# Routing of the expert layer: shifted, gained and transposed rows, positions and lists computed in another form and order

## The reference, cut to what matters

```python
h2 = rmsnorm(x, g_norm2) * (1.0 + sc2) + sh2
logits = h2 @ w_router + b_router              # 32 experts
top_logit, top_idx = lax.top_k(logits, 4)
gate = softmax(top_logit)
# every expert's tokens, padded to blocks of 128 slots:
padded = (counts + 127) // 128 * 128
slot = pad_start[expert] + rank of the token in its expert
slot_tok, slot_gate                            # lists, by slot
block_expert = searchsorted(pad_end, block_start, side='right')
y = swiglu(h_pad[tok] @ w_gate_up[e] + b_gate_up[e]) @ w_down[e] + b_down[e]   # a block
out[slot_tok] += y * slot_gate
```

## Time and profile before

| what | value |
|---|---|
| median of 3 runs | 2510.17 us |
| the profiled execution | 2509.06 us, its span 2507.2 us |
| TensorE busy | 2416.3 us, 96% of the span |
| VectorE busy | 2024.9 us, 81% |
| ScalarE busy | 1320.3 us, 53% |
| GpSimd busy | 678.6 us, 27% |
| granted TensorE clock, mean | 0.98 of full speed |
| moved by DMA | 572.48 MB, 228 GB/s |

### The profile page before, as it was taken

The page is one execution under the profiler, slowest core; times in us unless marked ns, Lnnn a source line. Parts: engine busy times, 40 slices in busy tenths (PEclk is TensorE's granted clock), DMA queues, the critical chain, the costliest instruction groups (busy, mean ns, idle before and its releaser), DMA issues.

```text
span 2507.2 us, 31686 instructions
## 1 busy us (share of the span) xinstructions
PE 2416.3 (96%) x10915; PEld 1944.6 (78%) x10915; DVE 2024.9 (81%) x1856; ACT 1320.3 (53%) x1206; POOL 678.6 (27%) x407
## 2 busy tenths in 40 slices
PE   8999999999999999999869999999999999999995
PEld 7777788786877877878657888888888888888884
DVE  7787577576885786885269999999999999999994
ACT  4442233334323234334247777777777777777772
POOL 5343341332433432341312122112111211221120
PEclk9999999999999999999879999999999999999997
DMA  6232245222422752230069999999999999999992
GB/s 237 84 125 77 67 152 185 67 76 72 147 68 76 267 208 72 69 100 1 13 240 363 378 365 371 368 377 364 367 367 377 366 366 373 371 368 366 377 358 88
DMA packets 104427, 572.48 MB, mean 228 GB/s; under 512 B 14192, under 2 KB 14336, under 8 KB 54288
## 3 DMA queue, kind: packets, MB, share of 16 engines
q1 hardware_dynamic: 86784, 515.15, 54.9%
q0 software_dynamic: 17280, 56.20, 7.9%
q10 hardware_dynamic: 288, 0.14, 0.0%
HBM read 559.37 MB, written 24.12 MB: 233 GB/s over the span
## 4 chain that ended last, share of the span: by engine, by line
PE 86%; DVE 7%; DVEq 2%; DMA 1%; ACT 1%; issue 1%; ACTq 0%; POOL 0%; SPq 0%; POOLq 0%
PE ps L1493 83%; PE ps L1171 2%; DVE scr L2354 1%; DVE scr L2194 1%; DMA scr<-in_ada 1%; DVEq L2356 1%; DVE y_split L2131 1%; PE ps L666 0%; DVE mix L2245 0%; DVE scr L2243 0%; DMA mix<-acc_rows 0%; PE ps L1423 0%; DVEq L2141 0%; DMA acc_rows<-rows,lst 0%; DVE w_split L1298 0%
## 5 line engine op out<-in xcount | busy, mean ns | idle before, releaser
L1298 DVE TENSOR_TENSOR w_split<-raw,w_split 128x2048 fp32r<-128x2048 f32 x386 | 877.3, 2287 | 54.3 <-ACT w_split L1250 43.3
L1493 PE MATMUL ps<-y_split,pieces_split 128*128 128x512 f32 x3600 | 844.6, 395 | 15.9 <-POOLq L2561 7.3
L1250 ACT ACTIVATE w_split<-raw 128x2048 fp32r<-128x2048 f32 x386 | 736.2, 1916 | 196.0 <-PE ps L1493 176.3
L1493 PEld LDWEIGHTS ps<-y_split,pieces_split 128*128 128x128 f32 x3600 | 679.9, 189 | 167.8 <-issue 26.1
L1493 PE MATMUL ps<-w_split,rows_T 128*128 128x512 f32 x3096 | 751.9, 393 | 1.9 <-DVE rows_T L1304 1.9
L1493 PEld LDWEIGHTS ps<-w_split,rows_T 128*128 128x128 f32 x3096 | 575.3, 188 | 119.4 <-DVE rows_T L1304 2.5
L2549 POOL TENSOR_TENSOR pieces_split<-pieces,pieces_split 128x1024 fp32r<-128x1024 f32 x151 | 372.3, 2476 | 646.4 <-ACT pieces_split L1827 518.5
L1827 ACT ACTIVATE pieces_split<-pieces 128x1024 fp32r<-128x1024 f32 x144 | 151.3, 1058 | 425.6 <-PE ps L1493 394.4
L1493 PE MATMUL ps<-w_split,hidden_T 128*128 128x512 f32 x1536 | 363.6, 392 | 2.0 <-DVE hidden_T L1304 1.7
L1493 PEld LDWEIGHTS ps<-w_split,hidden_T 128*128 128x128 f32 x1536 | 284.9, 188 | 74.6 <-DVE hidden_T L1304 15.0
L1362 POOL COPY rows_i<-slot_tokens 128x1 int32 (+1 forms) x34 | 60.9, 1790 | 412.9 <-PE ps L1171 379.4
(11 more groups left out here) (265 smaller groups left out, 2068.8 us busy)
## 6 DMA issues: line engine op xcount, KB each, us to landing
raw<-in_w_moe SPq DMA_DIRECT2D x386, 1024.0 KB, 7.6
pieces<-in_pieces SPq DMA_DIRECT2D x181, 512.0 KB, 3.6
scr<-in_ada POOLq DMA_DIRECT2D x48, 512.0 KB, 5.6
scr<-in_ple SPq DMA_DIRECT2D x2, 1536.0 KB, 6.9
acc_rows<-in_zeros POOLq DMA_DIRECT2D x5, 512.0 KB, 10.9
hT<-in_xT SPq DMA_DIRECT2D x8, 256.0 KB, 5.6
h_rows<-scr SPq DMA_DIRECT2D x4, 512.0 KB, 3.7
mix<-acc_rows SPq DMA_DIRECT2D x4, 512.0 KB, 5.1
```

Of the source, the lines that this page charges most:

```text
L1250: nc.scalar.activation(wsp[:, p % SPLIT, 0], raw[:, p % RAW, :], ACT.Copy).then_inc(high, 3 if p == 1 else 1)
L1298: nc.vector.tensor_tensor(wsp[:, p % SPLIT, 1], raw[:, p % RAW, :], wsp[:, p % SPLIT, 0].bitcast(F32), ALU.subtract).then_inc(low, 3 if p ...
L1493: return pe.matmul(out, lhsT, rhs, start=start, stop=stop)
```

## The change: what it does

- **Norm.** The rows are scaled by their gain alone (`gained`, ScalarE for tiles 0 to 6, VectorE for tile 7) as soon as each tile of `hT` is there. The norm's factor, which belongs to a token, is applied where tokens lie on partitions, on four columns (`r_col`): to the logits, and in the copy of the transposed rows. The squares of tiles 0 to 6 are added by VectorE, and TensorE sums two tiles by columns.
- **Logits.** Their products stand between the groups w4 to w7, those of tile 7 behind. The shift's share is a sum over the router's weights (`shifted_bias`).
- **Shift of the rows.** SP writes the shift to a row in DRAM, one element at a time, and copies this row to all 513 rows of `h2_rows`. GpSimd adds the rows to it with four accumulating DMAs in place of SP's four writes. Token numbers begin at 1, and row 0 serves the empty slots.
- **Transposes.** All eight half tiles are transposed ahead of the positions, over three PSUM banks. The exponentials follow behind the copies.
- **Positions and lists.** Positions take five wider products in place of fifteen, the blocks of a slot are found by rounding, the experts of the blocks by a column and one more product (group `be`), and place and owner of all 16 choices have buffers of their own. The lists' products are 100 columns wide in place of 150.
- **First block.** The first two gathers read their indices from the list itself, and the first block's rows are taken in two halves (`t_full`, `t_out` count one more).
- **Bias.** Its loads wait for w0 in place of w7, and `bias_act` stands behind the square of tile 4.

The core of the diff:

```diff
 def tail_sp(sp):
     for t in range(A_RAW, len(TAIL)):
+        if t == A_RAW + 2:
+            sp.wait_ge(csum_ready, 1)
+            sp.dma_start(shift_dram[0, :].rearrange("(k p) -> p k", p=P), ada[:, SH2:SH2 + DK, 0],
+                         allow_slow_non_contiguous=True).then_inc(h2_init, 16)
+        if t == A_RAW + 6:
+            sp.wait_ge(h2_init, 16)
+            sp.dma_start(h2_dram[:, :], shift_dram[0, :].partition_broadcast(ROWS)).then_inc(h2_init, 16)
 ...
-    for t in range(ST):
-        sp.wait_ge(h2n_ready, t + 1)
-        sp.dma_start(h2_dram[t * P:(t + 1) * P, :], h2n[:, t, :]).then_inc(h2_out, 16)
 def tail_pe(pe, mm):
+            def token_sums(tile, last):
+                for t in range(ST):
+                    m = mm(ps[:, 5, t:t + 1], sq3[:, tile, t * P:(t + 1) * P], ones[:, 0:1], False, last and t == ST - 1)
 ...
             for m_ in range(DK):
                 features(CV, f"w{m_}", ...)
-            sums(CA, "norm2", 8, DK)
+                if m_ == 4:
+                    mm(ps[:, 4, 0:ST * E_N], ident[:], zer.unsqueeze(1).to_broadcast([P, ST, E_N]), True, False)
+                    for k in range(4):
+                        pe.wait_ge(norm2_ready, GAINED(k))
+                        logits_of(k)
+                if m_ > 4:
+                    pe.wait_ge(norm2_ready, GAINED(m_ - 1))
+                    logits_of(m_ - 1)
+                if m_ == 6:
+                    pe.wait_ge(route_ready, SHIFT)
+                    mm(ps[:, 5, E_N:2 * E_N], ones[:], shift_sum, True, True).then_inc(route_full, 1)
+            pe.wait_ge(route_ready, SQ_SUM)
+            mm(ps[:, 5, 0:ST], ident[:], zer[:, 0:ST], True, False)
+            token_sums(0, False)
+            pe.wait_ge(norm2_ready, SQUARED(DK - 1))
+            token_sums(DK - 1, True)
+            pe.wait_ge(route_ready, LAST_GAINED)
+            logits_of(DK - 1)
+            for i in range(8):
+                turned_gained(i)
 ...
-            for t in range(ST + 1):
-                for t2 in range(min(t + 1, ST)):
-                    lhs = before[:] if t2 == t else ones[:]
-                    m = mm(ps[:, CV.bank(g), t * E_N:(t + 1) * E_N], lhs, chosen[:, t2, :], ...)
+            for d in range(1, ST + 1):
+                mm(ps[:, CV.bank(g), (d if d > 1 else 0) * E_N:(ST + 1) * E_N], ones[:],
+                   flat_[:, (d > 1) * E_N:(ST + 2 - d) * E_N], d == 1, False)
+            mm(ps[:, CV.bank(g), 0:(ST + 1) * E_N], before[:], flat_[:, E_N:(ST + 2) * E_N], False, True)
 ...
 def tail_act(act, ...):
             for k in range(DK):
-                shift(h2T[:, k, :], k, SH2, 0, n2_scaled, k + 1, h2_ready)
+                nc.scalar.activation(sq3[:, k, :], hT[:, k, :], ACT.Square)
+                if k < DK - 1:
+                    nc.scalar.activation(gained[:, k, :], hT[:, k, :], ACT.Copy, scale=coef[:, 2, k:k + 1])
+                if k == 4:
+                    bias_act(act)
+                if k == 6:
+                    nc.scalar.activation(small[:, 1:2], small[:, 0:1], ACT.Sqrt)
+            nc.scalar.activation(std_col, ps[:, 5, 0:ST], ACT.Sqrt, bias=EPSC, scale=1.0 / D)
 ...
 def tail_dve(dve, ...):
             for t in range(ST):
...
+                n0, n1 = t * TOP, (t + 1) * TOP
+                nc.vector.tensor_tensor(owner[:, n0:n1], in_block[:, n0:n1, :]..., value[:, n0:n1, :]..., ALU.mult)
+                nc.vector.tensor_tensor(place[:, n0:n1, :], cst[:, 0:P]..., rem[:, n0:n1]..., ALU.is_equal)
                 dve.drain().then_inc(onehot_ready, 1)
 ...
 def experts_pool(pool):
+            for t in range(ST):
+                pool.wait_ge(h2n_ready, t + 1)
+                pool.dma_start(h2_dram[1 + t * P:1 + (t + 1) * P, :], h2n[:, t, :], accum_op=ALU.add).then_inc(h2_out, 16)
             pool.wait_ge(h2_out, 16 * ST)
             pool.wait_ge(list_ready, 1)
-            fetch(0, 0)
-            fetch(1, 1)
+            rows_of(list_tok[:, 0:1], 0)
+            rows_of(list_tok[:, 1:2], 1)
```

More of the change, by code:

```diff
@@ L975, in tail_dve @@
             dve.sem_inc(CA.free, len(CA.banks))
+            nc.vector.memset(chosen[:, 0, :], 0.0)
+            nc.vector.memset(chosen[:, ST + 1, :], 0.0)
+            nc.vector.memset(zer, 0.0)
+            dve.drain()
             for m in range(DK):
@@ new lines, in tail_dve @@
+                if m == DK - 1:
+                    nc.vector.tensor_scalar(gained[:, m, :], hT[:, m, :], coef[:, 2, m:m + 1], None,
+                                            ALU.mult).then_inc(route_ready, 1)
+                elif m:
+                    dve.wait_ge(norm2_ready, SQUARED(m))
+                    m_ = nc.vector.tensor_tensor(sq3[:, 0, :], sq3[:, 0, :], sq3[:, m, :], ALU.add)
+                    if m == DK - 2:
+                        m_.then_inc(route_ready, 1)
+                    dve.drain()
@@ L984, in tail_dve @@
+            dve.wait_ge(std2_ready, 9)
+            nc.vector.reciprocal(r_col, std_col)
+            dve.drain().then_inc(route_ready, 1)
+            dve.wait_ge(route_full, LOGITS)
+            for t in range(ST):
+                nc.vector.scalar_tensor_tensor(logits[:, t, :], ps[:, 4, t * E_N:(t + 1) * E_N], r_col[:, t:t + 1],
+                                               shifted_bias, ALU.mult, ALU.add)
             dve.drain()
-            x = full(CV, "logits")[:, 0:ST * E_N].rearrange("p (t e) -> p t e", t=ST)
@@ L988, in tail_dve @@
-            nc.vector.tensor_tensor(logits, x, brt[:].unsqueeze(1).to_broadcast([P, ST, E_N]), ALU.add)
-            dve.drain().then_inc(CV.free, 1)
             for t in range(ST):
@@ L1001, in tail_dve @@
+            nc.vector.tensor_tensor(hk, cst[:, 0:E_N].unsqueeze(1).unsqueeze(1).to_broadcast([P, ST, TOP, E_N]),
                                     ixf[:, :, 0:TOP].unsqueeze(3).to_broadcast([P, ST, TOP, E_N]), ALU.is_equal)
             dve.drain()
[L1003 to L1007 removed]
@@ L1008, in tail_dve @@
-            dve.drain().then_inc(chosen_ready, 1)
-            x = full(CV, "pos")
-            nc.vector.tensor_copy(posn, x[:, 0:ST * E_N].rearrange("p (t e) -> p t e", t=ST))
-            count = x[:, ST * E_N:(ST + 1) * E_N]
-            nc.vector.tensor_scalar(nblk, count, 0.0, None, ALU.is_gt)
-            nc.vector.memset(zer, 0.0)
-            for t in range(1, ST):
-                dve.drain()
-                nc.vector.scalar_tensor_tensor(nblk, count, float(t * P), nblk, ALU.is_gt, ALU.add)
@@ L1018, in tail_dve @@
-            dve.drain().then_inc(CV.free, 1)
+            nc.vector.reduce_sum(chosen[:, 1:ST + 1, :], hot.rearrange("p (t k) e -> p t e k", k=TOP), AX.X)
+            dve.drain().then_inc(route_ready, 1)
+            nc.vector.tensor_tensor(gates, mx8[:, :, 0:TOP], mx8[:, :, 0:1].to_broadcast([P, ST, TOP]), ALU.subtract)
+            dve.drain().then_inc(gate_d, 1)
+            x = full(CV, "pos")
+            nc.vector.tensor_scalar(nblk, x[:, ST * E_N:(ST + 1) * E_N], (P - 1) / 2, 1.0 / P, ALU.add, ALU.mult)
@@ L1047, in tail_dve @@
             nc.vector.tensor_tensor(h2k, hk, posn.unsqueeze(2).to_broadcast([P, ST, TOP, E_N]), ALU.mult)
-            dve.drain()
+            nc.vector.tensor_scalar(be_bc[:], full(CV, "be", LISTS), float(E_N - 1), None, ALU.min)
+            dve.drain().then_inc(CV.free, 1)
+            nc.vector.tensor_copy(be_r[:], be_bc[0:1, :]).then_inc(be_ready, 1)
+            dve.sem_inc(low, 2)
             nc.vector.reduce_sum(slotf, hot2, AX.X)
@@ L1116, in bias_sp @@
         def bias_sp(sp):
-            sp.wait_ge(CV.full, CV.done(0, "w7"))
+            sp.wait_ge(CV.full, CV.done(0, "w0"))
             for i in range(2):
```

278 lines of the change are left out of this document (152 added, 126 removed).

## The result

The changed kernel takes 2474.07 us (median of four runs, 2472.93 to 2476.75), the kernel before 2510.01 in the same session. The ratio is 0.9858 with a 95% interval of 0.9841 to 0.9875: 36 us, or 1.4%, faster. Forecast were 2475.9. Two later sessions gave 0.9854 and 0.9859. Five more traces (`delay5`, `loads_held`, `warm`, `rows_together`, `plain_rows`) run the same code on TensorE, ScalarE and VectorE up to the positions, and there the positions start between 9.07 and 10.35 us behind E; the three have 8.85 to 9.33.

The account below looks back on a forecast made before the run. Routing between the dense parts is one serial path. First half at 1228.9 + 32.6 = 1261.5, not 1295.83, takes 34.3 us off 2509.06, giving 2474.8; with 1.1 for the median 2475.9, range 2468 to 2490.

Parts of the forecast that it names:

- Features: Output product stage: 60 small instructions added on TensorE at 0.11 us, +6.5 us, between 3 and 13; other moved work hidden.
- Norm and logits: From VectorE's last addition to hT through sums, root and last logits to `chosen`: 7.7 us.
- The clock rival: Clock falls behind VectorE's last addition to hT, small products cost 0.216 us: about +6, 2482 us; clock or products 10%.
- Positions: Eighth half tile transposed at 7.5, 0.2 us ahead of `chosen`; positions' products done and handed over at 9.2 us.
- the last rival: The eighth transpose, not `chosen`, releases the positions: at most 1 us, inside the range; no chance of its own.
- VectorE up to the lists: `be_r` at 12.7 us, one-hots from 15.2, 1.2 each, to 20.0; lists at half clock to 23.3, `list_ready` 24.2.
- Fetch: First gather: 0.75 us to its start, 4.2 to land, 1.0 charged for meeting SyncE's loads from 14.5: landed at 30.1.
- First half: One half tile transposed, copied and subtracted alone: 2.5 us, old 4.45; experts' first half at 32.6.
- Rows' way to memory: GpSimd's four accumulating DMAs overlap and land at 15 to 20 us, under the lists (24.2): priced at zero.
- the rival of accumulates that don't overlap: The four accumulating DMAs run in series, end 5.7 or 26 us late: 2480.6 or 2501 us; 8%, half near 2501.
- The two new DMAs on SyncE: Element write (12 us) and copy to 513 rows (6 to 10 us), hidden by 23 and 20.2 us of slack.
- The rival with all of them on one engine: Single-element write sits on one engine: 187 us, tail stops for 164, about 2640 us; 3%.

Follow-up runs that it names:

- delay5: Changed kernel with seven idle 512-column sums on VectorE behind the experts of the blocks, ahead of the one-hots: 2478.41 us, ratio to before 0.9872.
- loads_held: Changed kernel with SyncE's third and fourth weight loads held until the first gather has landed: 2475.77 us, ratio to before 0.9866.
- warm: Changed kernel with unread 512-column products on TensorE: 8 behind the positions, 19 ahead of the lists, 28 ahead of the first rows: 2472.69 us, ratio 0.9857.
- rows_together: Changed kernel with the first block's rows transposed, copied and subtracted as one 1024-column tile, not in halves: 2478.90 us, ratio to before 0.9876.
- plain_rows: Changed kernel with SyncE's plain row writes in place of GpSimd's four accumulating DMAs, the shift left out of the result: 2474.59 us.
- logits_behind: Changed kernel with the logits of tiles 0 to 6 moved behind w7, ahead of the norm's sums: 2479.64 us, ratio to before 0.9882.
- warm_front: As `warm`, with five more unread products between the first transposed half tiles: 2474.51 us, ratio to before 0.9857.

## Why the prediction was right, point by point

The mechanism held: one serial path, shortened, and what came off it came off the span. The total met the trace to 0.1 us, which is better than its steps were: the path behind E was forecast 1.9 us too short and E 1.1 too early, and the loop and end, forecast as unchanged, were 2.9 shorter. That these cancel is luck.

- **Features.** Forecast +6.5, measured +6.35, by two errors against each other. The prediction counts 60 small instructions ahead of E; only 52 stand there, since tile 6's eight follow w7. The 48 logits instructions cost 0.11 us each (logits experiment), 5.28 in all, and the zero product and the shift's sum 1.07 for four instructions, where 0.44 was charged. Not foreseen: beside GpSimd's work on the biases VectorE slows down, its addition to 4.66 us where such an addition takes 0.69, and then a copy of 16 columns to 1.83.

```profile
1222.30 3.52 POOL L1213 MEMSET rows<- 128x4096 f32 x1
```

```profile
1224.02 1.83 DVE L1079 COPY scr<-cst 128x16 f32<-128x16 f32 x1
```

  Both together pushed tile 6's addition to hT back by 3 us. It cost TensorE a wait of 0.22 us for the shift's sum at 1223.98 and nothing more, since tile 7 came 4.1 later.
- **Norm and logits.** `chosen` at 8.6, forecast 7.7; the terms that the prediction gives for it (3.4, 0.55 and 4.0) add up to 7.95. Tile 6's logits push the sums back, so the root starts at 2.8 and not 2.5. The clock rival happened here: 0.50 from E + 3.1 to E + 3.9 on, in all three traces of the changed kernel, for 3.4 us. It was priced at 6 us. In the last logits it cost 0.3 to 0.4 (1.32 and 1.47 us, 1.06 where it fell latest); the 32 transposing instructions, which also wait for banks, took 5.61 us, forecast 4.1; the ten of the positions ran at 1.00 again, in 1.4 us. In `warm`, `loads_held` and `rows_together`, alike up to there, it was low for 6.8 us and the positions stood at 10.3, 1.0 to 1.5 us later than in the three: so up to there the rival was worth at most the 2.5 us by which they came late, not 6. The sum over k took 1.06 us and not 0.75.
- **Positions.** At 9.2, forecast 7.8. The last rival, that the eighth transpose releases them, also happened: the row copies with a gain for each token are 0.67 to 0.73 apart, not 0.57, the very case for which the prediction had set 0.7 us. Two half tiles behind the positions take it away; its size is 0.5 to 0.6 in the three traces.
- **VectorE up to the lists.** Positions to `be_r` 4.8, forecast 4.9. The first one-hot stood at 18.0, forecast 16.4: 1.4 of that is inherited, and the four tiles stood 1.3 apart, not 1.2. Lists 6.45, forecast 6.9 at half clock; the stretch shows 0.53, and the warmed form has 4.94 at 1.00. `list_ready` 25.3, forecast 24.2.
- **Fetch.** The term whose reasons failed most: gather 5.60 us (5.58 and 6.21 in the two repeats), forecast 5.2 with 1.0 for the loads, and SyncE's first load at 18.2, forecast 14.5. Three ways of taking the meeting away give the same price: later gather 4.13, held loads 4.23, rows written plainly some 4. So the loads cost it about 1.4 us, 2 in a repeat, and more where more of them stand beside it (7.10, 9.66). The forecast had the loads start 3.7 us too early and so the overlap too short, and charged a full microsecond for each one of overlap: two errors against each other.
- **First half.** 2.63 from the landing of the rows to the products, forecast 2.5; before 4.45.
- **Rows' way to memory.** Priced at zero, and GpSimd did not wait for them, so the rival of accumulates that don't overlap fell in this order: they held the DMA engines until about E + 20 (203 GB/s from 1248 to 1250, 360 in the next 2 us), the late end of the 15 to 20 forecast. It is one rearrangement away: with the transposes behind, the last one lands 2.3 us past `list_ready`. Nor are they free: with plain writes `be_r` is followed by a load 2.4 us sooner and the way to the second block is 2.0 to 2.8 us shorter, in one trace. The step that failed is "under the lists (24.2), so I price it at zero": what lands under cover still holds the DMA engines, and the price is up to those 2 us.
- **The two new DMAs on SyncE.** In this trace the element write was issued at 976.32 and the copy of rows at 1025.04. The pair of rows with which I took a piece's slack belongs to a piece of the end of the tail, not to piece 11, so the slack was read at the wrong place. TensorE was busy in every microsecond of both stretches all the same:

```profile
984.00:988.00 4.00, 4.00 (x18) 3.15 (x17) 3.08 (x5) 2.74 (x5) 0.00 (x0) 1.00 0.92 38
...
1025.00:1034.00 9.00, 9.00 (x59) 7.96 (x58) 6.42 (x9) 3.15 (x5) 2.45 (x2) 1.00 0.62 235
```

  In the first the DMA engines are 92% busy for 38 GB/s, and between 970 and 1000 there are 1131 packets of under 512 B. The Trainium skill, page "DMA: Bandwidth & Descriptors", "Rules for kernel authors", has this write as one descriptor for each element; the share beside so few bytes agrees. The rival with all of them on one engine, 187 us, did not come: the small packets were over some 14 us after its issue; 12 was the forecast.
- **Loop.** Forecast unchanged, measured 2.2 us shorter, with first-block stalls of 2.09 and 1.73 us (before 2.38 and 1.73). Of the 2.2, 0.76 lies in the first block (50.41 against 51.17). The three traces of the changed kernel have 1161.06 to 1161.28 for the loop, so it is no scatter between them. With the rows taken together the first block is back at 51.54 and the loop some 0.9 us longer, so the halves account for the 0.76. There is one trace of before, and where the other 1.5 us lie is left open.

## What to carry to other kernels

Small products are cheap where the clock stays up: 0.11 us each here between dense ones, the same in a run of their own while the clock is at 1.00, and 0.216 at half; a run of 56 that began at full clock came to 0.14 each. On a serial path what reaches the first dense product reaches the span, but later steps can take up a part of a gain or a delay (2.96 of 5.3 us arrived). Before two steps are brought together, look at what they share: here the DMA engines took back 1.4 us of the gain, and up to 5.5 in another order. A transfer that lands in time is not free while its engines are wanted by the next; price what stands behind it in the queues too.

## What the runs showed of the hardware

- The granted clock fell between E + 3.1 and E + 3.9 in the three traces of the changed kernel, and at E + 2.5 to E + 2.8 in `warm`, `loads_held`, `rows_together` and `warm_front`, while TensorE had no idle time in its rows, with small products only (columns 1 to 128). Between 1125 and 1130 before, with 3.50 of 5 us busy, it stood at 1.00. With a product of 512 columns behind each tile's logits it stood at 1.00 until E + 8.6.
- Accumulating writes of rows of 4 KB, issued by GpSimd, moved 186 to 209 GB/s with the engines' share at 1.0 (stretches of 2 us); plain writes of the same rows, issued by SyncE, 320 GB/s with the share at 0.78. SyncE's first load came 4.1 us behind `be_r` beside accumulates and 1.6 without them. By which resource they hold it up, no run here shows.
- VectorE's 512-wide addition took 4.66 us beside GpSimd's subtraction and 0.69 without it, in all eleven traces that have this order there:

```profile
1215.37 6.80 POOL L1210 TENSOR_TENSOR bias_split<-rows,bias_split 32x3072 fp32r<-32x3072 f32 x1
```

  It began at 1218.06 and ended at 1222.72, 0.55 behind the end of GpSimd's; in the other ten traces it is 0.55 too. The copy of 16 columns ended at 1225.85, 0.03 behind GpSimd's clearing; in `logits_behind`, where it met the subtraction, it took 5.91 us and ended 0.04 behind it. The Trainium skill, page "SBUF — State Buffer", section "Who interferes with whom", has the pair of ports as a lock that whoever starts first holds for its whole instruction, and names VectorE's additions with both inputs in SBUF among those that meet GpSimd's reads; the two ends agree with that.
